# The second norm by rows inside the output projection and the lookup, with the first query weights loaded early; the expert loop of TensorE written out

## The reference, cut to what matters

```python
def rms_norm(x, g):
    y = xf * lax.rsqrt(jnp.mean(xf * xf, axis=-1, keepdims=True) + EPS)
    return (y * g.astype(jnp.float32)).astype(x.dtype)
...
    h = x + jnp.sum(gates * merged, axis=2) @ w_out
    y = h + peer_ffn(rms_norm(h, norm_ffn), peer_wq, peer_keys, peer_u, peer_v)
...
def peer_ffn(x, wq, keys, u_tab, v_tab):
        q = (xb @ wq).reshape(blk, PEER_HEADS, 2, PEER_DK)
        s = jnp.einsum('nhpd,hpkd->nhpk', q, keys)
        s1, i1 = lax.top_k(s[:, :, 0], PEER_TOPK)
        ...
        act = jax.nn.gelu(jnp.einsum('nhkd,nd->nhk', u_tab[idx], xb), approximate=False)
        return jnp.einsum('nhk,nhkd->nd', (g * act).astype(v_tab.dtype), v_tab[idx])
```

## Time and profile before

| What | us |
|---|---|
| median of 3 runs | 6589.6 (6586.34 to 6605.64) |
| the profiled execution, its own time | 6580.98 |
| its span, from the first to the last instruction | 6579.2 |
| TensorE busy in the span | 6209.3 (94%) |
| VectorE busy | 3589.2 (55%) |
| ScalarE busy | 2008.0 (31%) |
| granted TensorE clock, mean over the span | 0.969 |

### The profile page before, as it was taken

The page is one execution under the profiler, slowest core; times in us unless marked ns, Lnnn a source line. Parts: engine busy times, 40 slices in busy tenths (PEclk is TensorE's granted clock), DMA queues, the critical chain, the costliest instruction groups (busy, mean ns, idle before and its releaser), DMA issues. The chain is left out here.

```text
span 6579.2 us, 109006 instructions
## 1 busy us (share of the span) xinstructions
PE 6209.3 (94%) x42728; PEld 5824.8 (89%) x42728; DVE 3589.2 (55%) x6665; ACT 2008.0 (31%) x3074; POOL 0.7 (0%) x6
## 2 busy tenths in 40 slices
PE   8999988979999999999989999899799999999999
PEld 6777768979999989999967777689799999899999
DVE  3444353337788875555434443533377888755554
ACT  2223223222234442222222232232222344422222
POOL 0000000000000000000000000000000000000000
PEclk9999989989999999999999999899899999999999
DMA  3212212224346665454322122122243466654443
GB/s 103 70 49 75 70 38 77 76 98 123 112 129 187 180 195 211 167 183 168 130 99 70 50 74 71 37 82 72 103 122 114 127 189 185 195 205 178 172 169 136
DMA packets 494711, 804.30 MB, mean 122 GB/s; under 512 B 81716, under 2 KB 303156, under 8 KB 476212
## 3 DMA queue, kind: packets, MB, share of 16 engines
q1 hardware_dynamic: 494436, 800.67, 38.2%
HBM read 616.20 MB, written 186.72 MB: 122 GB/s over the span
## 5 line engine op out<-in xcount | busy, mean ns | idle before, releaser
L1664 PE MATMUL ps<-parts,wh 128*128 128x288 f32 x9216 | 1856.4, 297 | 41.6 <-DVE wl L1894 41.6
L1664 PEld LDWEIGHTS ps<-parts,wh 128*128 128x128 f32 x9216 | 1473.3, 188 | 44.8 <-DVE wl L1894 42.5
L1664 PE MATMUL ps<-parts,wl 128*128 128x288 f32 x4608 | 1356.7, 294 | 0.0
L2103 PE MATMUL ps<-parts,vh 128*128 128x320 f32 (+1 forms) x4096 | 886.8, 297 | 36.3 <-DVE gl L2175 32.1
L2103 PE MATMUL ps<-gl,vh 128*128 128x320 f32 (+1 forms) x4096 | 878.8, 295 | 0.0
L2103 PE MATMUL ps<-parts,vl 128*128 128x320 f32 (+1 forms) x4096 | 874.6, 294 | 0.0
L1664 PEld LDWEIGHTS ps<-parts,wl 128*128 128x128 f32 x4608 | 867.9, 188 | 0.0
L2180 DVE TENSOR_TENSOR vl<-third,vh 128x512 fp32r<-128x512 f32 x512 | 352.7, 689 | 677.7 <-ACT vh L2123 677.7
L2123 ACT CAST vh<-third 128x512 fp32r<-128x512 f32 x512 | 317.1, 620 | 1165.4 <-PE ps L2103 1136.7
L2103 PEld LDWEIGHTS ps<-parts,vh 128*128 128x128 f32 x4096 | 623.8, 188 | 48.9 <-issue 32.7
L2103 PEld LDWEIGHTS ps<-parts,vl 128*128 128x128 f32 x4096 | 631.4, 189 | 0.0
(11 more groups left out here) (376 smaller groups left out, 8010.2 us busy)
## 6 DMA issues: line engine op xcount, KB each, us to landing
raw<-in_u SPq DMA_DIRECT2D x256, 512.0 KB, 4.0
third<-in_v SPq DMA_DIRECT2D x512, 256.0 KB, 2.9
activated<-go SPq DMA_DIRECT2D x256, 288.0 KB, 4.3
coefficients<-wt SPq DMA_DIRECT2D x34, 2048.0 KB, 9.3
wr<-in_w_cm SPq DMA_DIRECT2D x104, 512.0 KB, 4.5
first<-activated SPq DMA_DIRECT2D x32, 1152.0 KB, 5.6
gb<-activated SPq DMA_DIRECT2D x32, 1152.0 KB, 6.0
wb<-coefficients SPq DMA_DIRECT2D x32, 1152.0 KB, 8.4
```

The costliest lines, as they stand in the source:

```text
L1664: last = nc.tensor.matmul(out, wp[:, slot, k, :], xp[:, k, cols], start=(k == 0 and wp is T.wh and xp is T.xh), stop=(k == KD - 1 and wp i ...
L2103: last = nc.tensor.matmul(out, vp[:, x % 4, m * P:(m + 1) * P], gp[:, row, col:col + size], start=begins, stop=False, skip_group_check=True)
```

## The change

Four edits.

1. `norm_stage` is gone. The squares and their sums are made in `out_stage`, row by row: ScalarE squares row k as soon as it has been added (`square`), and TensorE multiplies that row by the ones matrix behind the next product (`total`). ScalarE's table load stands at the start of `out_stage`, and Ln and Exp at its end. The scaling by the norm weight, the cast and the subtraction move into the start of `lookup_stage`, also row by row, through a ring of 4 rows (`scaled`). TensorE's first two lookup tiles are computed together there, row by row (`first_products`): for each row k, 12 matmuls for tiles 0 and 1.
2. The first four query weight tiles are loaded and three of them split within `out_stage`, into buffers that now live across both stages. The end of `out_stage` no longer waits for the store of `residual`; SyncE waits for it in `lookup_stage`, at tile 2.
3. In `hgrn_stage` the copy to `kt` moves from VectorE, behind the five masked sums, to ScalarE, ahead of the take of projection 5.
4. In `value_stage` TensorE's hardware loop of 8 passes is written out as straight code of 16 blocks. The loops of the other engines stay.

Tiles are placed anew for this: `h` and the squares lie in `wt` during the output stage, `wh` and `wl` are both in `splits`, and `gl` and the second `gb` reuse `splits` and `raw` in the value stage.

```diff
@@ hgrn_stage, scalar and vector
-            for u in range(2, 6):
+            for u in range(2, 5):
                 take(u)
+            act.wait_ge(s["turned"], 1)
+            nc.scalar.copy(T.kt[:], bank(T, 6, NP_).rearrange("p (t k) -> p t k", t=TILES)
+                           ).then_inc(s["keys_ready"], 1)
+            take(5)
...
-            dve.wait_ge(s["turned"], 1)
-            nc.vector.tensor_copy(T.kt[:], bank(T, 6, NP_).rearrange("p (t k) -> p t k", t=TILES)
-                                  ).then_inc(s["keys_ready"], 1)
@@ out_stage, sync
+            for n in range(WRING):
+                sp.dma_start(T.raw[:, n], T.d["w_query"][l, n]).then_inc(s["next_in"], 16)
             sp.wait_ge(s["added"], KD + 2)
...
-            sp.wait_ge(s["x_out"], 16)
+            sp.wait_ge(s["next_in"], 16 * WRING)
@@ out_stage, tensor
+            def total(k):
+                pe.wait_ge(s["squared"], k + 1)
+                for a in range(2):
+                    last = nc.tensor.matmul(bank(T, 4 + a)[:, 0:HALF], T.ones, T.sq[:, k % 4, a * HALF:(a + 1) * HALF],
+                                            start=(k == 0), stop=(k == KD - 1))
+                last.then_inc(s["summed"], 1)
...
                 last.then_inc(s["produced"], 1)
+                if n:
+                    total(n - 1)
+            total(KD - 1)
@@ out_stage, scalar
+            nc.scalar.preload_act_table_set(LOG_EXP)
...
+            def square(k):
+                act.wait_ge(s["added"], k + 3)
+                if k >= 4:
+                    act.wait_ge(s["summed"], k - 3)
+                nc.scalar.activation(T.sq[:, k % 4, :], T.h[:, k, :], ACT.Square).then_inc(s["squared"], 1)
...
             for n in range(2, KD):
                 high(n)
+                square(n - 2)
+            act.wait_ge(s["next_in"], 16 * WRING)
+            for n in range(LEAD):
+                nc.scalar.copy(T.wh[:, n], T.raw[:, n]).then_inc(s["next_high"], 1)
+            square(KD - 2)
+            square(KD - 1)
+            act.wait_ge(s["summed"], KD)
+            nc.scalar.activation(two(T.rsn), halves(T, 4), ACT.Ln, bias=T.eps, scale=1.0 / D).then_inc(s["scaled"], 1)
+            act.wait_ge(s["scaled"], 1)
+            nc.scalar.activation(T.rsn, T.rsn, ACT.Exp, scale=-0.5).then_inc(s["rooted"], 1)
@@ lookup_stage, tensor
-            for n in range(TILES_STATIC):
+            def first_products():
+                pe.wait_ge(s["low"], 2)
+                pe.wait_ge(s["drained"], 2)
+                for k in range(KD):
+                    pe.wait_ge(s["x_low"], k + 1)
+                    for n in range(2):
+                        for a in range(2):
+                            for wp, xp in ((T.wh, T.xh), (T.wh, T.xl), (T.wl, T.xh)):
+                                last = nc.tensor.matmul(bank(T, 2 * n + a)[:, 0:HALF], wp[:, n, k, :],
+                                                        xp[:, k, a * HALF:(a + 1) * HALF],
+                                                        start=(k == 0 and wp is T.wh and xp is T.xh),
+                                                        stop=(k == KD - 1 and wp is T.wl))
+                        if k == KD - 1:
+                            last.then_inc(s["used"], 1)
+
+            first_products()
+            scores(0)
+            for n in range(2, TILES_STATIC):
@@ lookup_stage, vector
+            scale(0)
+            scale(1)
+            for k in range(KD):
+                x_low(k)
+                if k + 2 < KD:
+                    if k >= 2:
+                        dve.wait_ge(s["x_low"], k - 1)
+                    scale(k + 2)
             for i in range(2):
                 last = nc.vector.memset(T.qt[i], 0.0)
@@ value_stage, tensor
-            with pe.Fori(0, BLOCKS // 2) as q:
-                for b in range(2):
-                    steps(2 * q + b, b)
+            for p in range(BLOCKS):
+                steps(p, p % 2)
```

More of the change, by code:

```diff
@@ L1557, in out_stage @@
 def out_stage(nc, T, l):
[L1559 to L1560 removed]
+    with stage(nc, "w_even", "w_odd", "x_in", "m_high", "m_low", "high", "low", "produced", "added", "squared", "summed",
+               "scaled", "rooted", "next_in", "next_high", "next_low", shared=T.bridge) as (block, s):
         w_in = (s["w_even"], s["w_odd"])
@@ L1629, in _ @@
                     low(n + 2)
+                if n == KD - 2:
+                    for i in range(LEAD):
+                        dve.wait_ge(s["next_high"], i + 1)
+                        nc.vector.tensor_tensor(T.wl[:, i], T.raw[:, i], T.wh[:, i].bitcast(F32), ALU.subtract
+                                                ).then_inc(s["next_low"], 1)
+            dve.wait_ge(s["next_low"], LEAD)
+            dve.wait_ge(s["added"], KD + 2)
 ROWS = 8
@@ new lines, in program @@
+                with ExitStack() as merging:
+                    wm = sb(merging, "wm", [P, 12, P])
+                    early = T.br[:, 0:3, :].rearrange("p a n -> p (a n)")[:, 0:12 * P]
+                    T.wm = (wm[:], early.rearrange("p (k c) -> p k c", k=12))
+                    T.wmh = sb(merging, "wmh", [P, 2, 12, P], F32R)
+                    T.wml = sb(merging, "wml", [P, 2, 12, P], F32R)
+                    T.brh = sb(merging, "brh", [P, 16, N], F32R, side="right")
+                    T.brl = sb(merging, "brl", [P, 16, N], F32R, side="right")
+                    T.mt = T.xn[:, :, 0:N]
+                    sg = sb(merging, "sg", [P, 3, N])
+                    T.sg = [two(sg[:, i, :]) for i in range(2)]
+                    T.ma = two(sg[:, 2, :])
+                    merge_stage(nc, T, l)
```

123 lines of the change are left out of this document (48 added, 75 removed).

## The result

The changed kernel took **6497.6 us** (median of 4 runs, 6493.6 to 6506.8) against 6588.0 us (6586.3 to 6605.6) on the same chip: a ratio of 0.9859, 95% interval 0.9847 to 0.9872, 90.4 us less. In the first set of experiments it took 6497.4 us against 6589.8 us over 17 runs of the kernel before (0.986, 0.9844 to 0.9875). The forecast was 6518 us and its range began at 6502. The sign held, the range missed the time by 4.4 us.

The account below looks back on a forecast made before the run. TensorE, busy for 94% of the span, was taken as the bound. Savings of 65.3 - 0.2 + 6.4 + 0 = 71.5 us took the profiled 6580.98 to 6509.5, a median of 6518 us; range for 8 in 10: 6502 to 6545.

Parts of the forecast that it names:

- The norm chain: From last output product to first scores: 28.5 us instead of 61.15, 32.6 less per layer, 65.3 us for two.
- The totals: Sums of squares in the output product stream: six ahead of the end of product 7 add 6.0 us.
- the barrier: Between output and lookup stages: one stage change remains, 1.3 us until VectorE's first instruction.
- the 96 matmuls: First two lookup tiles, row by row: 14.8 us, with 18 matmuls at half clock after about 5 us idle.
- the rival at half clock throughout: Start of lookup: all 96 matmuls at half clock, 23.3 us instead of 14.8, giving 6535 us; chance 10%.
- The table load: ScalarE's load moved ahead of the output stage's first casts: nearly covered, +0.1 us a layer, at worst 1.3.
- HGRN: Copy to `kt` moved to ScalarE: removes 8 TensorE waits of 0.80 us, 6.4 us, called the most it could be.
- the one gap of 20 us: TensorE's idle stretch of 20.70 us before the first lookup product; the clock after it served to price the new start.
- The written-out loop: Value stage as straight code: 0 us, with some 43 more instruction packets a layer.
- The rival of the jump: Value loop: each of 14 jumps back costs 1.07 us, so writing out gives 15 us more, 6503 us; chance 5%.
- my slower rival, straight code that starves TensorE: Value stage: 87 instruction packets exposed by 1.07 us each, 93 us, giving 6611 us, slower than before; chance 5%.
- From the profiled execution to the median: Whole kernel: the median of three lay 8.6 us above the profiled execution, so 6509.5 became 6518 us.

Follow-up runs that it names:

- Parts 5 and 6: Kernel before with VectorE's copy to `kt` made twice, 6615.6 us; kernel before with three unread float32 matmuls in TensorE's wait for that copy, 6569.5 us.
- part 2: Changed kernel with TensorE's hardware loop of 8 passes put back in the value stage: 6626.4 us, ratio 1.0054.
- the second kernel of part 3: Kernel before with 208 more instructions (met waits) on TensorE just ahead of the value loop: 6689.5 us, ratio 1.0153.
- the first kernel of part 3: Changed kernel with the value loop kept and 48 more instructions (met waits) on TensorE ahead of it: 6495.6 us, ratio 0.9851.

## Why the prediction was too small

**The norm chain: right.** 65.3 us were forecast, 64.7 were found. The totals put the products 7.32 us apart (7.36 forecast); from the last product to the scores it was 22.3 us (28.5 - 6.0 = 22.5). The single terms held too: the barrier 1.24 (1.3), the idle time before the lookup 5.2 (about 5), the 96 matmuls 14.34 (14.8), with the clock at half for the start of them and not throughout. The early weights carry 12.5 us of it and the order by rows 8.3 by the medians (12.8 by the trace), measured one by one. One figure beside the sum was off: the rival at half clock throughout should have had 2 x 12.7 = 25.4 us and not 23.3, some 4 us more for both layers.

**The table load: hidden.** TensorE's wait ahead of the first output product is the same in both kernels, first before, then changed, so the forecast 0.2 us did not come:

```profile
PE ps L1587 <- DVE wol L1614: 17.1, 2, 8.6
PE ps L1560 <- DVE wol L1608: 17.1, 2, 8.6
```

**HGRN: the step that failed.** "6.4 us, the most it could be" took the wait for the whole price. Measured were 14.1 and 22.6 us by the runs and 19.2 by the mixers' length in the traces. The shorter stages are 7.8 to 9.2 of it. The rest is that TensorE's clock fell to half behind this wait in 8 of 40 stages, for 9.5 us a time, and in none of 104 without it. Parts 5 and 6 show it from both sides: a wait made 6.9 us longer costs 26 us, a wait filled with useless work gives 18.6. The profiled execution that the prediction was read from has none of these stretches in its HGRN stages, so rows of them were not at hand, but a sign was: its mixers ran at a mean granted clock of 0.97 from 30 to 900 us, its value stage at 1.00. I priced the clock at the one gap of 20 us and nowhere else, and gave this term no upper end.

**The written-out loop: the price was right, the question was not.** Straight code costs nothing (0 forecast; 0.9995 measured in the kernel before), 42 packets a layer are hidden. The rival of the jump had its weight from the page "Runtime: NRT & Kernel Launch" of the Trainium skill, section "Instruction fetch mechanics", by which a taken branch to a target outside the fetched window stalls. The loop of the kernel before gave no such stall, but I took that for a property of the loop. It was one of its place: where the rest of the change puts it, 8 instructions earlier by my count, each jump costs 9.2 us, and writing it out avoids 129 us. With that rule the traces of part 2 and of the second kernel of part 3 agree (9 packets a jump), and those of the kernel before and of the first kernel of part 3 do not (none). Priced against the kernel before the edit is worth nothing, as forecast; without it the change would have been a loss of 0.5%. That case was missing from my list: my slower rival, straight code that starves TensorE, did not come about.

**The value stage: a term that was missing.** The new steps give 6.9 us, by exclusion through the tiles' new places. I had listed the placement as part of the change and priced it at nothing without saying so.

**From the profiled execution to the median: the same step again.** I added 8.6 us, since the median lay above the profiled execution. The profile of after lies 3.8 us above its median instead. So of the 20.5 us by which the forecast was high, 12.4 stand here; the other 8.1 are what the change gave between the two profiled executions (79.6) beyond the sum, mainly 2.8 from the HGRN stages (9.2 instead of 6.4) and 6 to 7 from the value stage. The profiled execution of before was a lucky one: no half-clock stretch behind the wait for `kt`, where the other four kernels with that wait had one to three. The change removes them, so the distance to the median should not have been carried over. The kernel before scatters from 6574 to 6605 us over 17 runs, with granted clocks from 0.970 to 0.964 in step; the changed kernel from 6494 to 6500 over 4.

**The sum again.** 64.7 + 14 to 22.6 + 6.9 = 85.6 to 94.2 us, around the 90.4 and 92.3 that were measured.

**What stays open.** Why a tile's start changes the pace of matmuls by 0.4 to 1%, and by which rule. Why the clock falls behind the wait for `kt` in some executions and not in others; as it does so in 0 to 3 of 8 stages, the 22.6 us in one kernel and the 14.1 in the other can't be told from the 19.2 of the traces. And where instruction packets begin, and why a jump brings 9 of them where the loop by my count touches seven or eight.

## What to carry to other kernels

Price a wait of TensorE by the clock too: where the mean granted clock around a short wait is below 1, the wait can cost two to four times its length, as this one did, and filling it with products that nothing reads is a quick test of that. One profiled execution can miss it; look at the same place in the traces of several kernels. A long hardware loop can be free or cost microseconds a pass by where its code lies; when a change adds or removes instructions ahead of it, compare the count of instruction packets with that of before, and if it grew with the passes, write the loop out or move it. Take the distance of equal steps in the trace before and after: it separates a steady pace (placement) from waits and clock, and it repeats to a nanosecond where medians scatter by ten microseconds.

## What I had not expected of the hardware

- A jump back of the same loop cost 9.2 us, and nothing once 48 instructions that do nothing stood ahead of the loop; the costly form fetched 9 more instruction packets a jump.
- Instructions of two waits that are met at once start 106 ns apart on TensorE; 208 of them, partly in the cover of another wait, delayed it by 15 us a layer.
- Shifting one tile by 64 bytes changed 24 matmuls from 3160.0 to 3147 ns, or in the kernel before from 3173.4 to 3140, with TensorE busy all through. With two other shifts groups of eight steps alternated between 3120 ns and 3173 or 3200.
- Behind a wait of 0.8 us TensorE's clock fell to half for 20 us in 8 of 40 stages. Three useless products in that wait made the whole kernel 18.6 us faster (0.9972, 0.9961 to 0.9984).
